# A hybrid decoder layer on one core: the order of the first loads, and eight opening weight halves run as two sweeps over four banks

## The chip, the core and the metric

The kernel runs on one core of one Trainium2 chip. The metric is the device time of one execution in microseconds (us); of several executions the median is taken. Engines are named as in the profile: PE is TensorE, DVE VectorE, ACT ScalarE, POOL GpSimd, SP SyncE. SP computes nothing here; it issues nearly all of the transfers, in the order of its program. Loads are counted in MiB of 1,048,576 bytes.

## The reference, cut to what matters

One layer over 256 tokens of width 2048, all float32. A vector c makes six modulation vectors of 2048 through the matrix `w_mod`; two of them (shift and scale) act on the normalized x ahead of the first projection:

```python
c_act = jax.nn.silu(c)
mod = (c_act @ w_mod[l] + b_mod[l])[:, None, :]
sh1, sc1, g1, sh2, sc2, g2 = jnp.split(mod, 6, axis=-1)
h = rms_norm(x, norm1_g[l]) * (1.0 + sc1) + sh1
(fq, fk, fv, ff, nq, kc, vc, ksl, vsl, kwn, vwn, ng, ca, cg) = split_in(h @ w_in[l])
...
x = x + g1 * (mixed @ w_out[l])
h = rms_norm(x, norm2_g[l]) * (1.0 + sc2) + sh2
x = x + g2 * (jnp.square(jax.nn.relu(h @ w_mlp1[l])) @ w_mlp2[l])
return rms_norm(x, final_g)
```

`mixed` joins two attentions and a convolution. The change touches the program up to the first part of `h @ w_in`.

## The kernel before

Float32 products are made of three matmuls on split operands. Each operand is the sum of a high part (rounded, ACT makes it) and a low part (the rest, DVE makes it): high times high, high times low, low times high.

**Weights.** The columns of `w_in` stand in eleven groups of 512 (CA, CG, FV, FE, NQ, NS, NC, FA, FB, FC, and a narrow TL). A quarter is 512 rows of a group, one load of 1 MiB into one of four buffers `raw0` to `raw3`. A half is half of a quarter, 256 rows: ACT writes its high part to one of four `w_hi` (`weight_hi`, L637), DVE its low part to one of four `w_lo` (`weight_lo`, L1288), and PE runs 24 matmuls on it (`feature_rows`, L891 to L893, or `token_rows`, L914 to L916). In the text, h0, h1, ... are the halves in PE's order. `UNITS` lists which quarters follow each other into the same accumulator. There are four of these, bank pairs `pair[0]` to `pair[3]`. The first four units are quarter 0 of CA, CG, FV and FE, one in each pair, so that h0 and h1 are both halves of the first quarter of CA, h2 and h3 of CG, and so on. ACT may convert half n when PE has done half n - 4 (`pe_half`).

**Modulation.** A chunk m of `w_mod` is 1 MiB and gives 128 numbers: DVE multiplies it with the activated c and sums over a row (`modulation_column`, L1295). Chunks 0 to 3 make shift and scale of the first 256 features of h, chunks 4 to 7 of the next 256. Chunks 0 to 7, here m0 to m7, are loaded into the `raw` buffers ahead of all weights. Later ones (m8 and on) go to two buffers `mod_raw`, and DVE works them off between its weight halves at the turns that `MODS_AT` lists. Every engine walks over one list of turns. At turn n ACT and DVE prepare half n, and PE, three slots later in its own list, multiplies it. DVE's turns 7 and 8, in order: low part of h7, m11, m12; then a small memset and the low parts of h8 and h9.

**h.** ACT squares x (L618), DVE makes the inverse root (`inverse_rms`), ACT scales x (L625), PE transposes it in eight blocks through two PSUM banks (L979) and ACT copies each block out (`xn_t`, L629). For each 256 features ACT then applies shift and scale and makes the high part (`scale_shift`, L648 and L651) and DVE the low part (`split_h`, L1345). h0 needs the first such piece, h1 the second.

**Loads.** SP waits on semaphores before it issues a load whose buffer is in use: for m4 to m7 and the first four quarters on `mod_step`, which counts the chunks that DVE has done; for later quarters on `lo_done`, which counts the halves that DVE has split; for later chunks on `mod_step` again. A load that waits holds up all that stand behind it on SP. Ten small constants are issued by ACT (L605). ACT also writes the table of relative positions to DRAM (`bias_rows`, L660) at turn 5 and waits for its arrival before its first copy of a result (`copy_result`, L666).

## Time and profile before

| | |
|---|---|
| median of 3 executions | 1260.14 us (1258.65 to 1262.6) |
| the profiled execution | 1256.01 us |
| its span, first to last instruction | 1254.3 us, so 1.7 us lie around it |
| PE / weight loads of PE / DVE / ACT busy | 93% / 81% / 72% / 48% |
| mean granted clock of PE | 0.971 of 2.4 GHz |

A busy share is a mean over the whole layer. The change lies in the first 70 us, where PE has its longest idle stretches, so the windows of those 70 us and what ends each wait in them matter more than the totals.

### The profile page before, as it was taken

Reading aid. Unit: us, or ns where it says so; the run is one execution under the profiler, and the core shown is the slowest. Engines: PE = TensorE matmul, PEld = TensorE weight load, DVE = VectorE, ACT = ScalarE, POOL = GpSimd, SP = SyncE. Lnnn points to the kernel's source line nnn. Section 1 sums busy time; section 2 is a strip of 40 time slices with the busy share of each in tenths; the row PEclk is TensorE's granted clock in tenths of the full one; section 3 lists DMA queues with packets and bytes.
Section 4 is the critical chain, followed back from the end, with each engine's and each line's share of the span. In section 5 each row is a group of like instructions: output and inputs, shape, how many; then the busy total and the mean of one; then the engine's idle time right before and its main releaser. Section 6 shows DMA issues by size and latency. Waiting matters only on the chain.

```text
span 1254.3 us, 17205 instructions
## 1 busy us (share of the span) xinstructions
PE 1160.6 (93%) x6775; PEld 1014.0 (81%) x6775; DVE 903.1 (72%) x1009; ACT 597.7 (48%) x858; POOL 8.6 (1%) x24
## 2 busy tenths in 40 slices
PE   2789999898998998599999999999999999999995
PEld 1789998887876777599988888888888888888784
DVE  5788898999998867698766567554576545667674
ACT  5554546875645543544434344434444433444442
POOL 2000000000000000000000000000000000000000
PEclk9899999899898999799999999999999999999998
DMA  9999998456875556298576655556565556664441
GB/s 367 416 368 370 364 383 346 156 200 239 310 240 206 230 196 242 102 377 338 221 270 234 247 224 205 196 202 231 208 256 184 191 201 226 243 234 168 168 168 67
DMA packets 45913, 307.17 MB, mean 245 GB/s; under 512 B 6349, under 2 KB 7961, under 8 KB 9241
## 3 DMA queue, kind: packets, MB, share of 16 engines
q1 hardware_dynamic: 42768, 303.50, 64.5%
q10 hardware_dynamic: 3016, 2.78, 0.8%
q8 instruction: 43, 0.70, 0.2%
q14 instruction: 22, 0.17, 0.0%
q0 software_dynamic: 64, 0.02, 0.0%
HBM read 304.16 MB, written 2.12 MB: 244 GB/s over the span
## 4 chain that ended last, share of the span: by engine, by line
PE 72%; DVE 14%; issue 5%; ACT 5%; DMA 3%; ACTq 0%; SPq 0%; DVEq 0%
PE quad L901 14%; PE quad L914 11%; PE quad L916 11%; PE quad L915 11%; PE quad L903 7%; PE quad L891 5%; PE quad L892 5%; PE quad L893 5%; DVE w_lo L1288 3%; DVE mod_raw L1295 2%; DVE conv_y L1382 2%; DMA mod_raw<-in_w_mod 2%; ACT w_hi L637 2%; DMA raw<-in_w_mod 1%; ACT score L688 1%
## 5 line engine op out<-in xcount | busy, mean ns | idle before, releaser
L1288 DVE TENSOR_TENSOR w_lo<-raw,w_hi 128x1024 fp32r<-128x1024 f32 (+1 forms) x376 | 450.5, 1207 | 276.3 <-ACT w_hi L637 276.0
L637 ACT ACTIVATE w_hi<-raw 128x1024 fp32r<-128x1024 f32 (+1 forms) x376 | 391.8, 1046 | 464.6 <-PE quad L916 237.1
L901 PE MATMUL quad<-act,w_hi 128*128 128x512 f32 x768 | 271.5, 399 | 0.0
L891 PE MATMUL quad<-act,w_hi 128*128 128x256 f32 x768 | 225.2, 293 | 15.9 <-DVE w_lo L1288 10.7
L892 PE MATMUL quad<-act,w_hi 128*128 128x256 f32 x768 | 222.1, 289 | 0.0
L893 PE MATMUL quad<-act,w_lo 128*128 128x256 f32 x768 | 221.9, 289 | 0.0
L903 PE MATMUL quad<-act,w_lo 128*128 128x256 f32 x768 | 215.7, 281 | 0.0
L914 PE MATMUL quad<-w_hi,u_hi 128*128 128x512 f32 x512 | 199.6, 390 | 0.0
L915 PE MATMUL quad<-w_lo,u_hi 128*128 128x512 f32 x512 | 199.2, 389 | 0.0
L916 PE MATMUL quad<-w_hi,u_lo 128*128 128x512 f32 x512 | 199.2, 389 | 0.0
L901 PEld LDWEIGHTS quad<-act,w_hi 128*128 128x128 f32 x768 | 144.3, 188 | 36.0
L891 PEld LDWEIGHTS quad<-act,w_hi 128*128 128x128 f32 x768 | 152.6, 199 | 19.8 <-issue 14.8
L892 PEld LDWEIGHTS quad<-act,w_hi 128*128 128x128 f32 x768 | 152.4, 198 | 0.1
L893 PEld LDWEIGHTS quad<-act,w_lo 128*128 128x128 f32 x768 | 152.1, 198 | 0.0
L903 PEld LDWEIGHTS quad<-act,w_lo 128*128 128x128 f32 x768 | 145.1, 189 | 0.1
L1295 DVE CUSTOM_DVE_ANT_0 mod_raw<-mod_raw,acc 128x2048 f32<-128x2048 f32 x56 | 128.0, 2286 | 11.4 <-DMA mod_raw<-in_w_mod 11.1
L914 PEld LDWEIGHTS quad<-w_hi,u_hi 128*128 128x128 f32 x512 | 96.1, 188 | 20.3 <-issue 0.2
L915 PEld LDWEIGHTS quad<-w_lo,u_hi 128*128 128x128 f32 x512 | 96.1, 188 | 20.0 <-issue 0.2
L916 PEld LDWEIGHTS quad<-w_hi,u_lo 128*128 128x128 f32 x512 | 96.1, 188 | 19.9
L1306 DVE SCALAR_TENSOR_TENSOR acc<-mod_raw,c_act,acc 128x2048 f32<-128x2048 f32 x32 | 75.0, 2345 | 0.2 <-DMA mod_raw<-in_w_mod 0.2
L688 ACT ACTIVATE score<-score,neg_max 128x128 f32<-128x128 f32 x72 | 31.9, 444 | 51.6 <-DVE neg_max L1410 51.6
L676 ACT ACTIVATE conv_p<-conv_in,convw 128x256 f32<-128x256 f32 x108 | 45.8, 496 | 9.0 <-DVE conv_y L1382 9.0
(257 smaller groups left out, 1081.0 us busy)
## 6 DMA issues: line engine op xcount, KB each, us to landing
raw<-in_w_main SPq DMA_DIRECT2D x184, 1024.0 KB, 4.8
mod_raw<-in_w_mod SPq DMA_DIRECT2D x88, 1024.0 KB, 6.5
...
out<-raw SPq DMA_DIRECT2D x4, 512.0 KB, 4.0
...
```

The lines of the kernel that those rows point to most:

```text
L637: A(w_hi[j % 4][:, 0:2 * width], block_half(raw, j, width), ACT.Copy).then_inc(hi_done, 1)
L891: mm(out, hi, act_hi[:, k, :], start=begin and m % 2 == 0, stop=False, skip_group_check=True)
L892: mm(out, hi, act_lo[:, k, :], start=False, stop=False, skip_group_check=True)
L893: last = mm(out, lo, act_hi[:, k, :], start=False, stop=end, skip_group_check=True)
L901: mm(out, w_hi[j % 4][:, cols], act_both[:, k, :, :].rearrange("p h t -> p (h t)"), start=begin, stop=False, skip_group_check=True)
L903: last = mm(out[:, 0:S], w_lo[j % 4][:, cols], act_hi[:, k, :], start=False, stop=end, skip_group_check=True)
L914: mm(out, t_hi, hi, start=begin, stop=False)
L915: mm(out, t_hi, lo, start=False, stop=False)
L916: last = mm(out, t_lo, hi, start=False, stop=end)
L1288: TTn(w_lo[j % 4][:, 0:2 * width], block_half(raw, j, width), w_hi[j % 4][:, 0:2 * width].bitcast(f32), ALU.subtract).then_inc(lo_done, 1)
L1295: v.tensor_tensor_reduce(out=src[:, :], in0=src[:, :], in1=acc[0][:, :], scale=1.0, scalar=0.0, op0=ALU.mult, op1=ALU.add, accum_out=m_col ...
L1306: STT(out, src[:, :], c_act[:, bass.ds(k, 1)], out, ALU.mult, ALU.add).then_inc(mod_step, 1)
```

## The change

Four things are changed together.

- **Order of the first loads.** SP issues the row of c, m0 and m1 (now into `mod_raw`), x, m2 and m3 (into `raw2` and `raw3`), the first halves of quarters 0 and 1 (0.5 MiB each), the ten small constants (moved from ACT), then m4, first half 2, m5, first half 3, m6, and the second halves of quarters 0 to 3 around m7. After these come m8 and m9.
- **Two sweeps.** The first eight halves go over the four bank pairs twice: h0 to h3 are now the first halves of CA, CG, FV and FE and need only the first piece of h. h4 to h7 are their second halves and need the second. The results of the four units are now copied at turns 8 to 11 (before: 5, 7, 9, 11), and the table of positions is written ahead of them.
- **x.** It is squared as each of its two row tiles arrives, and scaled and transposed in two halves of its features; the second four blocks are transposed between h1 and h2.
- **DVE and ACT orders** for m0 to m7 and h0 to h3 are written out by hand. A quarter 4 to 7 is issued when the low part of h4 to h7, each the last user of its buffer, is made. m8, m9 and m10 are worked off at turns 4, 5 and 6, m11 and m12 still at turn 7.

```diff
+HALF_AT[0:8] = [(n % 4, n // 4) for n in range(8)]
+UNIT_END = [5 + u if u < 4 else FIRST_HALF[u + 1] for u in range(N_UNITS)]
+FIRST_MODS = 4
+RAW_LOADS = (1, 1, 2, 2)
...
-MODS_AT = {2 * q + 1: 1 + (q in (3, 8)) for q in range(30) if q != 14}
+MODS_AT = {4: 1, 6: 1} | {2 * q + 1: 1 + (q in (3, 8)) for q in range(2, 30) if q != 14}
...
-            def weights_in(n):
-
-                sp.wait_ge(mod_step, MOD_FIRST - 4 + n + 2)
-                sp.dma_start(raw[n][:, :], main_d[n, :, :]).then_inc(raw_full[n], 16)
+            def first_part(n):
+
+                if n in (2, 3):
+                    sp.wait_ge(mod_step, n + 2)
+                sp.dma_start(first_half(n), main_d[n % 4, :, n // 4 * 2 * GW:(n // 4 + 1) * 2 * GW])\
+                    .then_inc(part_in[n] if n < 4 else raw_full[n - 4], 16)
 
             def modulation(m, slot):
 
-                if not (isinstance(m, int) and m < MOD_FIRST + 2):
-                    sp.wait_ge(mod_step, m)
+                sp.wait_ge(mod_step, m - 2 if isinstance(m, int) and m < 6 else m)
...
+            sp.dma_start(c_col[:, :], c_d).then_inc(c_in, 16)
             sp.dma_start(acc[0][:, :], crow_d.to_broadcast([P, D])).then_inc(c_in, 16)
-            sp.dma_start(c_col[:, :], c_d).then_inc(c_in, 16)
-            sp.dma_start(n1[:, :], n1_d).then_inc(c_in, 16)
-            sp.dma_start(b_col[:, :], bcol_d).then_inc(c_in, 16)
+            for m in range(2):
+                sp.dma_start(mod_raw[m][:, :], wmod_d[m, :, :]).then_inc(mod_full[m], 16)
             for tt in range(TT):
-                sp.dma_start(x_a[:, tt, :], x_d[tt * P:(tt + 1) * P, :]).then_inc(x_in, 16)
-            for m in range(MOD_FIRST):
-                if m >= 4:
-                    sp.wait_ge(mod_step, m - 4 + 2)
-                sp.dma_start(raw[m % 4][:, :], wmod_d[m, :, :]).then_inc(raw_full[m % 4], 16)
+                sp.dma_start(x_a[:, tt, :], x_d[tt * P:(tt + 1) * P, :]).then_inc(x_in[tt], 16)
+            sp.dma_start(n1[:, :], n1_d).then_inc(col_in, 16)
+            sp.dma_start(b_col[:, :], bcol_d).then_inc(col_in, 16)
+            for m in range(2, 4):
+                sp.dma_start(raw[m][:, :], wmod_d[m, :, :]).then_inc(raw_full[m], 16)
+            first_part(0)
+            first_part(1)
+            loads = [(n2[:, :], n2_d),
...
+            for dst, src in loads:
+                sp.dma_start(dst, src).then_inc(small_in, 16)
+            modulation(4, 0)
+            first_part(2)
+            modulation(5, 1)
+            first_part(3)
+            modulation(6, 0)
+            first_part(4)
+            modulation(7, 1)
+            for n in range(5, 8):
+                first_part(n)
+            for n in range(2):
+                modulation(MOD_FIRST + n, n)
...
-                sp.wait_ge(lo_done, 2 * (r - 4) + 2)
+                sp.wait_ge(lo_done, r + 1 if r < 8 else 2 * (r - 4) + 2)
...
-                if half is not None and half % 2:
+                if half is not None and 4 <= half < 8:
+                    next_quarter(half)
+                elif half is not None and half >= 8 and half % 2:
...
+            def scale_x(half):
+
+                act.wait_ge(rstd_ok, 1)
+                cols = slice(half * (D // 2), (half + 1) * (D // 2))
+                for tt in range(TT):
+                    A(x_a[:, tt, cols], x_a[:, tt, cols], ACT.Copy, scale=rstd[:, tt:tt + 1]).then_inc(xn_ok, 1)
...
-                act.wait_ge(pe_half, FIRST_HALF[u + 1])
+                act.wait_ge(pe_half, UNIT_END[u])
...
-            for b in range(2):
-                scale_shift(b)
-                weight_hi_in(b)
+            scale_x(0)
+            copy_x(0)
+            copy_x(1)
+            first_hi(0)
+            scale_shift(0)
+            first_hi(1)
+            copy_x(2)
+            copy_x(3)
+            first_hi(2)
+            scale_x(1)
+            first_hi(3)
+            for b in range(4, 8):
+                copy_x(b)
+            bias_rows()
+            scale_shift(1)
...
-            pe.wait_ge(xn_ok, TT)
-            for b in range(KT // 2):
+            def x_transposes(b):
+
+                pe.wait_ge(xn_ok, 2 if b < 4 else 4)
...
+            for b in range(4):
+                x_transposes(b)
...
                 if slot == 2:
 
+                    for b in range(4, 8):
+                        x_transposes(b)
                     pe.wait_ge(small_in, 16 * N_SMALL)
                     mm(spare[0:NNSA, 0:S], rel_t[:, :], onehot[:, :], start=True, stop=True).then_inc(bias_ps, 1)
-                if slot == FIRST_HALF[2]:
                     pe.wait_ge(xt_ok, KT // 2)
-                if slot == FIRST_HALF[3]:
+                if slot == 3:
...
-            for m in range(MOD_FIRST):
-                if m == 2:
-                    inverse_rms(0)
-                modulation_column(m, raw[m % 4], raw_full[m % 4], 16 * (m // 4 + 1))
-                if m % 4 == 3:
-                    scale_shift(m // 2 - 1, 2, m + 1, n1, m // 2 - 1)
+                if n < 8:
+                    dve.wait_ge(hi_done, n + 1)
+                    TTn(w_lo[n % 4][:, :], first_half(n), w_hi[n % 4][:, :].bitcast(f32), ALU.subtract)\
+                        .then_inc(lo_done, 1)
+                else:
+                    weight_lo(n // 8, n % 8, TAIL if n < IN_HALVES and UNITS[HALF_AT[n][0]][0] == TL else GW)
+
+            modulation_column(0, mod_raw[0], mod_full[0], 16)
+            modulation_column(1, mod_raw[1], mod_full[1], 16)
+            inverse_rms(0)
+            modulation_column(2, raw[2], raw_full[2], 16)
+            modulation_column(3, raw[3], raw_full[3], 16)
+            dve.wait_ge(col_in, 2 * 16)
+            scale_shift(0, 2, 4, n1, 0)
+            weight_lo_in(0)
+            split_h(0)
+            weight_lo_in(1)
+            modulation_column(4, mod_raw[0], mod_full[0], 32)
+            weight_lo_in(2)
+            modulation_column(5, mod_raw[1], mod_full[1], 32)
+            weight_lo_in(3)
+            modulation_column(6, mod_raw[0], mod_full[0], 48)
+            modulation_column(7, mod_raw[1], mod_full[1], 48)
+            scale_shift(2, 2, 8, n1, 2)
+            split_h(1)```

DVE at its start, where the first weight half follows the modulation chunks (`w_lo` is a weight's low part, `act` the low part of h, and ISA rows are a chunk's product and its read-out). Before:

```order
L1320 TENSOR_TENSOR m_sum<-m_col,b_col 128x4
L1321 SCALAR_TENSOR_TENSOR scale_h<-m_sum,n1 128x2
L1345 TENSOR_TENSOR act_49<-h_f0_63,act_49 128x2x256
L1288 TENSOR_TENSOR w_lo0<-raw0,w_hi0 128x1024
L1345 TENSOR_TENSOR act_49<-h_f1_64,act_49 128x2x256
L1288 TENSOR_TENSOR w_lo1<-raw0,w_hi1 128x1024
L1295 ISA mod_raw0,m_col<-mod_raw0,acc0 128x2048
```

And now, from the first sum of four chunks on:

```order
L1373 TENSOR_TENSOR m_sum<-m_col,b_col 128x4
L1374 SCALAR_TENSOR_TENSOR scale_h<-m_sum,n1 128x2
L1404 TENSOR_TENSOR w_lo0<-raw0,w_hi0 128x1024
L1398 TENSOR_TENSOR act_49<-h_f0_63,act_49 128x2x256
L1404 TENSOR_TENSOR w_lo1<-raw1,w_hi1 128x1024
L1348 ISA mod_raw0,m_col<-mod_raw0,acc0 128x2048
L1348 ISA m_col 128x1
L1404 TENSOR_TENSOR w_lo2<-raw2,w_hi2 128x1024
```

In the rows of before the sum is that of m4 to m7, in the rows of now that of m0 to m3: h0's low part stands ahead of four chunks that it used to follow, and m4 (the first ISA row of now) stands behind the low part of h1.

SP around the first weights, before:

```order
L490 DMA raw2<-in_w_mod 128x2048
L490 DMA raw3<-in_w_mod 128x2048
L472 DMA raw0<-in_w_main 128x2048
L478 DMA mod_raw0<-in_w_mod 128x2048
L472 DMA raw1<-in_w_main 128x2048
L478 DMA mod_raw1<-in_w_mod 128x2048
L472 DMA raw2<-in_w_main 128x2048
L472 DMA raw3<-in_w_main 128x2048
L499 DMA raw0<-in_w_main 128x2048
L478 DMA mod_raw0<-in_w_mod 128x2048
```

And now, from first half 3 on (128x1024 is a half of a quarter):

```order
L483 DMA raw3<-in_w_main 128x1024
L489 DMA mod_raw0<-in_w_mod 128x2048
L483 DMA raw0<-in_w_main 128x1024
L489 DMA mod_raw1<-in_w_mod 128x2048
L483 DMA raw1<-in_w_main 128x1024
L483 DMA raw2<-in_w_main 128x1024
L483 DMA raw3<-in_w_main 128x1024
L489 DMA mod_raw0<-in_w_mod 128x2048
L489 DMA mod_raw1<-in_w_mod 128x2048
L531 DMA raw0<-in_w_main 128x2048
L489 DMA mod_raw0<-in_w_mod 128x2048
L531 DMA raw1<-in_w_main 128x2048
```

The second row of now is m6, which waits for m4's buffer; the second halves, m7, m8 and m9 stand behind it.

DVE at turns 7 and 8, now (before, the same rows stand in the same order under their old line numbers):

```order
L1404 TENSOR_TENSOR w_lo3<-raw3,w_hi3 128x1024
L1348 ISA mod_raw1,m_col<-mod_raw1,acc0 128x2048
L1348 ISA m_col 128x1
L1373 TENSOR_TENSOR m_sum<-m_col,b_col 128x4
L1374 SCALAR_TENSOR_TENSOR scale_h<-m_sum,n1 128x2
L1348 ISA mod_raw0,m_col<-mod_raw0,acc0 128x2048
L1348 ISA m_col 128x1
L1592 MEMSET conv_in_70 128x4x30
L1341 TENSOR_TENSOR w_lo0<-raw0,w_hi0 128x1024
```

The product in the sixth row is m12, and h8's low part in the last row stands behind it, as it did before.

## Rows read from the trace of the kernel before

**Rows 1.** Page of the profile: span; busy us (share) and instructions by engine
```profile
span 1254.3 us, 17205 instructions
PE 1160.6 (93%) x6775; PEld 1014.0 (81%) x6775; DVE 903.1 (72%) x1009; ACT 597.7 (48%) x858; POOL 8.6 (1%) x24
```

**Rows 2.** Windows: busy us (instructions) of PE, PEld, DVE, ACT, POOL; PEclk, DMA share, GB/s
```profile
30.00:40.00 10.00, 3.65 (x20) 2.97 (x20) 8.47 (x12) 7.14 (x12) 0.00 (x0) 0.68 1.02 423
40.00:50.00 10.00, 10.00 (x67) 9.44 (x67) 8.20 (x8) 3.44 (x4) 0.00 (x0) 0.81 1.01 420
60.00:70.00 10.00, 6.60 (x30) 5.48 (x29) 8.00 (x10) 5.10 (x8) 0.00 (x0) 0.89 0.98 382
80.00:90.00 10.00, 10.00 (x86) 10.00 (x85) 8.12 (x10) 6.63 (x9) 0.00 (x0) 1.00 0.94 338
...
68.00:71.50 3.50, 3.50 (x18) 3.50 (x19) 3.30 (x4) 0.00 (x0) 0.00 (x0) 0.54 0.95 379
```

**Rows 3.** Chain that ended last, up to h8: start us, us, what
```profile
27.85 7.58 DMA raw<-in_w_main
...
37.92 0.55 PE quad L891
...
57.58 6.52 DMA mod_raw<-in_w_mod
66.59 1.24 DVE w_lo L1288
```

**Rows 4.** Timeline, DVE: start us, us, what, [idle before <-releaser]
```profile
13.81 2.29 DVE L1295 CUSTOM_DVE_ANT_0 raw<-raw,acc 128x2048 f32<-128x2048 f32 x1 [3.65 <-DMA raw<-in_w_mod]
19.22 0.16 DVE L1326 TENSOR_REDUCE newton<-ssq 128x2 f32<-128x8 f32 x1
20.64 0.16 DVE L1334 TENSOR_TENSOR rstd<-rstd,newton 128x2 f32<-128x2 f32 x1
64.12 2.29 DVE L1295 CUSTOM_DVE_ANT_0 mod_raw<-mod_raw,acc 128x2048 f32<-128x2048 f32 x1 [1.69 <-DMA mod_raw<-in_w_mod]
```

**Rows 5.** Timeline, ACT: same columns
```profile
12.27 0.61 ACT L618 ACTIVATE sq_a<-x_a 128x512 bf16<-128x512 f32 x1
20.84 3.90 ACT L625 ACTIVATE x_a<-x_a,rstd 128x2048 f32<-128x2048 f32 x2 [1.02 <-DVE rstd L1334]
26.00 0.60 ACT L629 ACTIVATE xn_t<-quad 128x512 f32<-128x512 f32 x1 [1.27 <-PE quad L979]
26.85 0.60 ACT L629 ACTIVATE xn_t<-quad 128x512 f32<-128x512 f32 x1 [0.26 <-PE quad L979]
36.42 1.08 ACT L648 ACTIVATE h_f<-xn_t,m_sum,scale_h 128x256 f32<-128x256 f32 x2
38.07 1.04 ACT L637 ACTIVATE w_hi<-raw 128x1024 fp32r<-128x1024 f32 x1
40.42 2.00 ACT L637 ACTIVATE w_hi<-raw 128x1024 fp32r<-128x1024 f32 x2 [1.31 <-DMA raw<-in_w_main]
45.40 1.06 ACT L637 ACTIVATE w_hi<-raw 128x1024 fp32r<-128x1024 f32 x1 [2.98 <-DMA raw<-in_w_main]
52.11 1.02 ACT L666 ACTIVATE conv_in<-quad 128x1024 f32<-128x1024 f32 x1 [4.59 <-DMA bias_scratch<-bias_p]
```

**Rows 6.** Timeline, SP's issues; then us from issue to landing (source of L478)
```profile
55.37 0.33 SPq L499 DMA_DIRECT2D raw<-in_w_main  x1
57.58 0.33 SPq L478 DMA_DIRECT2D mod_raw<-in_w_mod  x1
DMA to landing us min/median/max: 5.2/7.1/12.3
```

**Rows 7.** Timeline, PE: the last matmul of h7 and the first of h8
```profile
64.17 0.39 PE L916 MATMUL quad<-w_hi,act 128*128 128x512 f32 x1
67.96 0.55 PE L891 MATMUL quad<-act,w_hi 128*128 128x256 f32 x1 [3.40 <-DVE w_lo L1288]
```

**Rows 8.** Page, issues: KB of each, median us from issue to landing
```profile
out<-raw SPq DMA_DIRECT2D x4, 512.0 KB, 4.0
```

More of the change, by code:

```diff
@@ L336, in build @@
         c_in = sem("c_in")
+        col_in = sem("col_in")
+        part_in = [sem(f"part_in{i}") for i in range(4)]
         small_in = sem("small_in")
-        x_in = sem("x_in")
+        x_in = [sem(f"x_in{i}") for i in range(TT)]
         consts = sem("consts")
@@ L613, in _, with copy_x @@
             sqrt_table(0)
-            act.wait_ge(x_in, 16 * TT)
-            for n in range(4 * TT):
-                tt, cg = n % TT, n // TT
-                A(sq_a[:, n * GW // 2:(n + 1) * GW // 2].bitcast(mybir.dt.bfloat16),
-                  x_a[:, tt, cg * GW:(cg + 1) * GW], ACT.Square, accum_out=ssq[:, 0, tt, cg:cg + 1])\
-                    .then_inc(act_sq, 1)
+            for tt in range(TT):
+                act.wait_ge(x_in[tt], 16)
+                for cg in range(4):
+                    n = 4 * tt + cg
+                    A(sq_a[:, n * GW // 2:(n + 1) * GW // 2].bitcast(mybir.dt.bfloat16),
+                      x_a[:, tt, cg * GW:(cg + 1) * GW], ACT.Square, accum_out=ssq[:, 0, tt, cg:cg + 1])\
+                        .then_inc(act_sq, 1)
             act.wait_ge(dve_ms, 1)
             A(root[:, :], mean_sq[:, :], ACT.Sqrt).then_inc(act_root, 1)
-            act.wait_ge(rstd_ok, 1)
-            for tt in range(TT):
-                A(x_a[:, tt, :], x_a[:, tt, :], ACT.Copy, scale=rstd[:, tt:tt + 1]).then_inc(xn_ok, 1)
-            for b in range(KT // 2):
+            def scale_x(half):
+                act.wait_ge(rstd_ok, 1)
+                cols = slice(half * (D // 2), (half + 1) * (D // 2))
+                for tt in range(TT):
+                    A(x_a[:, tt, cols], x_a[:, tt, cols], ACT.Copy, scale=rstd[:, tt:tt + 1]).then_inc(xn_ok, 1)
+            def copy_x(b):
                 act.wait_ge(xt_ps, b + 1)
@@ L630, in _, with first_hi @@
                   ACT.Copy).then_inc(xt_ok, 1)
+            def first_hi(n):
+                act.wait_ge(part_in[n], 16)
+                A(w_hi[n][:, :], first_half(n), ACT.Copy).then_inc(hi_done, 1)
             def weight_hi(g, j, width=GW):
[L634 to L636 removed]
+                act.wait_ge(raw_full[j // 2], (g + RAW_LOADS[j // 2]) * 16)
+                act.wait_ge(pe_half, g * 8 + j - 3)
                 A(w_hi[j % 4][:, 0:2 * width], block_half(raw, j, width), ACT.Copy).then_inc(hi_done, 1)
             def weight_hi_in(n):
[L640 removed]
+                if n < 8:
+                    act.wait_ge(raw_full[n % 4], 16 * RAW_LOADS[n % 4])
+                    act.wait_ge(pe_half, n - 3)
+                    A(w_hi[n % 4][:, :], first_half(n), ACT.Copy).then_inc(hi_done, 1)
+                else:
+                    weight_hi(n // 8, n % 8, TAIL if n < IN_HALVES and UNITS[HALF_AT[n][0]][0] == TL else GW)
             def scale_shift(b):
                 act.wait_ge(col_ok, b + 1)
+                act.wait_ge(xt_ok, b + 1)
                 if b >= 2:
@@ L971, in _ @@
             pe.wait_ge(consts, 1)
-            pe.wait_ge(xn_ok, TT)
-            for b in range(KT // 2):
+            def x_transposes(b):
+                pe.wait_ge(xn_ok, 2 if b < 4 else 4)
                 if b >= 2:
@@ L1219, in normalized @@
                 half = 1 if b < KT // 4 else 2
-                pe.wait_ge(xn_ok, TT + half)
+                pe.wait_ge(xn_ok, 2 * TT + half)
                 pe.wait_ge(xn_act, half)
@@ L1309, in later_modulation @@
                 n = m - MOD_FIRST
-                source = (mod_raw[n % 2], mod_full[n % 2], 16 * (n // 2 + 1))
+                source = (mod_raw[n % 2], mod_full[n % 2], 16 * (n // 2 + 4))
                 if MOD_G1 <= m < MOD_H2:
@@ L1517, in _ @@
             for turn, (half, step) in enumerate(TURNS):
-                if turn < 2:
-                    split_h(turn)
+                if turn < FIRST_MODS:
+                    continue
                 if turn == 8:
@@ L1530, in _ @@
                 for u in ADDED:
-                    if turn == FIRST_HALF[u + 1] + 3:
+                    if turn == UNIT_END[u] + 3:
                         add_result(u)
```

39 lines of the change are left out of this document (15 added, 24 removed).

## The prediction

> **What bounds the kernel now.** I read the page first, then the windows of the first 80 us, the chain of waits up to h8, and last the timelines of DVE, ACT, SP and PE in that stretch.
>
> The page says that PE is busy for 93% of 1254.3 us [rows 1], so a change of the start can only win what PE idles there. Its first weight matmul starts at 37.92 [rows 3], and it idles again from the end of h7 (64.17) to h8 at 67.96 [rows 7]. From h8 on it is full: 86 matmuls in 10 us at 80 us, which is 24, one half, in 2.8 us [rows 2]. All the work behind h8 is the same before and after. So the change is worth what it moves the start of h8, plus what the clock does around it.
>
> What sets h8? In the chain the last steps ahead of it are a transfer into `mod_raw`, issued at 57.58 and landed 6.5 us later, and h8's low part at 66.59 [rows 3]. That transfer is m12: DVE stands idle until it lands at 64.12, multiplies it, and only then splits h8 [rows 4]. From m12's landing to PE's h8 it is 3.84 us.
>
> And what sets m12? The transfers share the DMA engines, whose share is 1.01 or 1.02 from 30 to 50 us at 420 to 423 GB/s [rows 2]. ACT's waits show the pace. The row of c, two tiles of x, m0 to m7 and quarter 0 are 12 MiB, and the 12th lands at 35.4 [rows 3]; m8 and quarter 1 (14) by 40.42, m9 and quarter 2 (16) by 45.40 [rows 5]. That is 2.49 us per MiB. m0, the 4th, lands at 13.81 [rows 4]; eight more at 2.49 would make 33.7, so 1.7 us are lost on the way. m12 is the 23rd: at 2.49 from the 12th it would land at 62.8, and it landed at 64.12. The missing 1.3 us follow an SP that had issued quarter 6 only at 55.37 and m12 at 57.58 [rows 6].
>
> **The change, part by part.** After the change the loads up to m12 are again the row of c, x, m0 to m12, eight halves of quarters (4 MiB) and quarters 4 to 6: 23 MiB. Nothing is removed ahead of m12, and DVE's h8 still stands behind it. PE's earlier h0 is therefore worth nothing by itself. The term that decides is whether the queue of transfers runs dry more or less often than before, so I walk through it.
>
> *Up to h0.* x's second tile is the 5th MiB and lands at 13.8 + 2.49 = 16.3. Its four squares, 0.61 each [rows 5], end at 18.8; the inverse root took 19.22 to 20.80, 1.6 us [rows 4], so 20.4. Half of x is scaled in 3.90 / 2 = 1.95: 22.4. Before, the first block's copy began 1.3 us after the scaling and the next 0.85 after that [rows 5]: 23.7 and 24.5, done 25.1. h0's high part, 1.06: 26.2 (its 0.5 MiB, number 7.5, landed at 22.5). m2 and m3 are done by 20.4 + 2 x 2.2 + 0.6 for the sums = 25.4. Shift, scale and high part took 36.42 to 38.07, 1.65 us [rows 5]: 27.8. DVE's low part, 0.7, lets PE begin h0 at 28.6, 9.3 us earlier than now.
>
> *First pause.* ACT makes h1's high part by 28.9, DVE its low part (1.24 [rows 3]) by 30.1 and then m4 by 32.3. m6 needs m4's buffer and is issued at 32.3. The 11 MiB issued ahead of it have landed by 13.8 + 7 x 2.49 + 1.7 = 33.0, and no load of this kind lands less than 5.2 us after its issue [rows 6]. So m6, the 12th, lands at 37.5, where an unbroken queue gives 35.5: 2.0 us lost. All later loads stand behind m6 on SP. How long the ten constants, now in SP's own queue, hold it is shown by no row; anything from nothing to about 2 us is hidden here, as m6's time comes from DVE and not from the queue. I take the 1.7 of before.
>
> *Second pause.* m7 lands at 41.2, m8 at 47.5, m9 at 50.0 (numbers 13.5, 16, 17); their issues, at 35.7, 39.7 and 43.4, are in time. m7 is done at 43.4, the sums at 43.9, ACT's second piece at 45.6, h4's high part at 46.7 and its low part at 47.9. Only then is `raw0` free, since h0 and h4 share it now, and quarter 4 is issued, 7.5 us later than before. It lands at 47.9 + 5.2 = 53.1, where the queue could have had it at 52.5: 0.6 us.
>
> *To m12.* Five more MiB (m10, quarter 5, m11, quarter 6, m12) put m12 at 53.1 + 12.5 = 65.6. The issues are in time: m10 at 50.1, quarter 5 at 51.3, m11 at 53.5, quarter 6 at 54.7, m12 at 57.9. Of the 1.3 us that m12 lost before I have replaced the cause by the second pause but not the thinner rate (382 GB/s from 60 to 70 us [rows 2]). Between 0 and 1.3 more I take 0.5, nearer to 0, as m12 now stands behind a longer queue: 66.1. h8 follows at 66.1 + 3.84 = 69.9 to 70.0, against 67.96: **+2.0 us**.
>
> *Hidden edits.* The copies of results at turns 8 to 11 lie on ACT while h8 waits for m12. The transposes of the last four blocks now stand between h1 and h2 on PE, some 3.4 us at 0.85 per block. With a low clock in h0 and h1 (5.6 us each from 28.6) they end by 43.2, with a recovering one by 41; ACT needs them before its second piece of h, which waits for m7's sums until 43.9 anyway. That cover is thin: each us beyond it delays quarter 4 and h8 by as much. The early table of positions frees ACT of a wait of 4.6 us at turn 5 [rows 5]; it delayed h5 to h7 and quarter 6, and is part of the 1.3.
>
> *Clock.* PE is done with h7 near 62.0 (h7's low part 59.1, one half 2.8), so it idles 8 us before h8, not 3.4. After 3.4 idle us the grant was 0.54 of 2.4 GHz from 68.0 to 71.5 [rows 2], so low for 3.2 us, a loss of 1.6. At the first weights, after a longer rest, it stayed low from 37.9 to 43.8 (0.81 over 40 to 50 is 3.8 us at half speed [rows 2]), a loss of 2.9. So this costs between 0 and 1.3 us more. I take 0, from the row of the same place, and keep 1.3 for the range.
>
> **Sum.** 1256.0 (the profiled execution) + 2.0 = 1258.0. The median of the runs shown is 4.1 above that execution, so the forecast is 1260.1 + 2.0 = 1262.1.
>
> **A rule of the skill.** The half loads are 0.5 MiB. The 512 KB stores at the end land in 4.0 us [rows 8] and a 1 MiB load at the least in 5.2: 1.2 for 0.5 MiB, the pace of the queue, and 2.8 that don't shrink. If each of the four extra transfers paid 2.8 in the queue, m12 would land 11 us later: 1273. Against it: full loads already land 2.49 apart, with no such part between them. The Trainium skill (DMA: Bandwidth & Descriptors, section Bandwidth) asks for transfers of at least 1 MiB for most of the peak rate; by that rule this rival would have its cause, while the trace's queue agrees with it only for a lone transfer.
>
> **The rivals.**
> - *The queue never pauses.* If m4 is done sooner than I walk, or the engines are still busy when m6 comes, m12 lands at 62.8 and h8 starts 1.3 us earlier than now; a clock that doesn't fall gives 1.6 more. 1257.2 to 1259.5. For it: DMA's share is full in the windows of before. Against it: m6's issue hangs on eight steps of ACT and DVE.
> - *The early start is kept.* If m12 is not bound by bytes but by DVE's turn, h8 follows h7 and up to 9.3 us are won: 1250.8. It decides from the point where 23 MiB could be there by 55 us; at 423 GB/s they alone take 57 us. Even a part beyond 3.8 us would need it.
> - *Late chain and cold clock.* ACT's steps to h1 run 1 to 2 us longer than the sum, m12 loses its full 1.3 again and the clock its 1.3: 1264 to 1266.5.
>
> **How the numbers follow.** Forecast case 0.48; no pause 0.15; early start kept 0.08; late chain and clock 0.25; half loads paying their own 0.04. A measurement here tells about 0.3%, 3.8 us, from no change, so the first two are "same": 0.63. Faster 0.08, slower 0.29. The range leaves out the early start, the half loads and the ends of the others: 1258.0 to 1266.0.
>
> **What the new profile would show.** PE's first weight matmul near 28.6; m6 issued near 32.3 with a dip of the transfer rate at 31 to 34 and a smaller one near 49; DVE idle ahead of m12, landing near 66; h8 near 70, after some 8 idle us of PE; from there the same rows as before, 2 us later. The prediction is wrong if DVE doesn't wait for m12, if the rate shows no dip, or if the time behind h8 is no longer that of before.

## The result: 0.3% slower, and where the profile after shows it

The changed kernel takes 1263.42 us (median of 22 runs, 1260.2 to 1272.36), the kernel before 1259.51 on the same chip (22 runs, 1257.53 to 1264.07). The ratio is 1.0029, 95% interval 1.0018 to 1.0040: by it 3.65 us more, 2.3 to 5.0. I had forecast 1262.1, 2.0 more, in a range of 1258 to 1266. The sign came, and so did the two pauses of the queue and the wait for m12; the size was too small.

The page of the profile after, first the span, then busy us and instructions by engine (against [rows 1]):

```profile
span 1264.6 us, 17222 instructions
PE 1165.7 (92%) x6775; PEld 1017.4 (80%) x6775; DVE 903.6 (71%) x1009; ACT 598.1 (47%) x860; POOL 8.6 (1%) x24
```

This span is 10.3 us longer than that of before, far more than the medians differ. The chain that ended last shows the first piece of it (start us, us, what; against [rows 3]):

```profile
32.05 5.73 DMA mod_raw<-in_w_mod
...
40.13 9.42 DMA mod_raw<-in_w_mod
...
51.90 7.24 DMA mod_raw<-in_w_mod
...
61.49 7.58 DMA mod_raw<-in_w_mod
...
71.56 1.24 DVE w_lo L1341
```

Before, one transfer into `mod_raw` stood in this stretch of the chain; now there are four, m6, m8, m10 and m12. Each is issued when DVE has worked off the chunk two before it (m4, m6, m8, m10), and DVE then waits for it. The stage has become a loop of two buffers. PE's timeline after (against [rows 7]), with the idle time ahead in brackets:

```profile
28.39 0.39 PE L938 MATMUL quad<-act,w_hi 128*128 128x256 f32 x1 [2.34 <-DVE act L1398]
48.55 0.35 PE L938 MATMUL quad<-act,w_hi 128*128 128x256 f32 x1 [3.91 <-DVE w_lo L1404]
62.75 0.47 PE L961 MATMUL quad<-w_hi,act 128*128 128x512 f32 x1 [3.24 <-DVE w_lo L1404]
72.93 0.55 PE L938 MATMUL quad<-act,w_hi 128*128 128x256 f32 x1 [5.60 <-DVE w_lo L1341]
152.79 0.36 PE L938 MATMUL quad<-act,w_hi 128*128 128x256 f32 x1 [0.74 <-DVE w_lo L1341]
```

h0 starts 9.5 us earlier than before and h8 5.0 us later. Between them lie two new waits (3.91 and 3.24), a longer one ahead of h8 (5.60 against 3.40) and the transposes that now stand behind h1. SP's timeline and DVE's landings (the same columns) show two pauses of the queue, and a start of it that is held up:

```profile
18.21 2.42 SPq L511 DMA_DIRECT2D pos_t<-in_pos  x2
20.68 0.61 SPq L489 DMA_DIRECT2D mod_raw<-in_w_mod  x1
...
32.05 0.33 SPq L489 DMA_DIRECT2D mod_raw<-in_w_mod  x1
...
48.43 0.33 SPq L531 DMA_DIRECT2D raw<-in_w_main  x1
...
61.49 0.33 SPq L489 DMA_DIRECT2D mod_raw<-in_w_mod  x1
```

```profile
37.81 2.29 DVE L1348 CUSTOM_DVE_ANT_0 mod_raw<-mod_raw,acc 128x2048 f32<-128x2048 f32 x1 [1.30 <-DMA mod_raw<-in_w_mod]
41.72 2.29 DVE L1348 CUSTOM_DVE_ANT_0 mod_raw<-mod_raw,acc 128x2048 f32<-128x2048 f32 x1 [1.61 <-DMA mod_raw<-in_w_mod]
49.57 2.29 DVE L1348 CUSTOM_DVE_ANT_0 mod_raw<-mod_raw,acc 128x2048 f32<-128x2048 f32 x1 [1.17 <-DMA mod_raw<-in_w_mod]
59.16 2.29 DVE L1348 CUSTOM_DVE_ANT_0 mod_raw<-mod_raw,acc 128x2048 f32<-128x2048 f32 x1 [2.81 <-DMA mod_raw<-in_w_mod]
69.09 2.29 DVE L1348 CUSTOM_DVE_ANT_0 mod_raw<-mod_raw,acc 128x2048 f32<-128x2048 f32 x1 [2.27 <-DMA mod_raw<-in_w_mod]
```

The ten constants keep SP until m4's issue at 20.68; m6 goes out at 32.05 and lands at 37.81, m7 lands at 41.72, m8 at 49.57, m10 at 59.16, m12 at 69.09.

How much is that? The last column of the windows is the rate at which bytes moved. Times the length of a window it is a count of bytes, and this count is what I compare most below. Before:

```profile
0.00:28.00 28.00, 3.12 (x15) 2.78 (x16) 15.12 (x22) 15.18 (x27) 6.31 (x22) 1.00 0.92 360
28.00:48.00 20.00, 13.65 (x77) 12.04 (x76) 18.47 (x19) 11.97 (x18) 0.00 (x0) 0.74 1.02 421
48.00:60.00 12.00, 11.66 (x71) 10.11 (x70) 6.08 (x7) 7.19 (x8) 0.00 (x0) 1.00 1.01 412
0.00:60.00 60.00, 28.44 (x159) 24.92 (x160) 39.67 (x46) 34.33 (x52) 6.31 (x22) 0.91 0.97 391
```

After:

```profile
0.00:28.00 28.00, 3.60 (x16) 2.96 (x16) 14.36 (x21) 16.38 (x31) 6.32 (x22) 1.00 0.90 351
28.00:48.00 20.00, 15.75 (x90) 13.50 (x90) 14.69 (x16) 11.79 (x17) 0.00 (x0) 0.91 0.98 378
48.00:60.00 12.00, 10.70 (x60) 9.43 (x60) 8.02 (x8) 6.39 (x8) 0.00 (x0) 0.86 0.91 345
0.00:60.00 60.00, 30.06 (x166) 25.89 (x166) 37.08 (x43) 34.56 (x54) 6.32 (x22) 0.94 0.93 359
```

By 60 us the changed kernel has moved (391 - 359) x 60 = 1.9 MB less. At the full queue's 420 GB/s [rows 2] that is 4.6 us: 0.6 of it up to 28 us, 2.0 from 28 to 48 (the first pause), 1.9 from 48 to 60 (the second). h8 is 5.0 us late. Further on, h35 (27 halves behind h8; every profile has a short wait ahead of it) starts at 152.79, against 148.09 in the profile before: 4.7 late.

### The profile page after: what moved, and what is told of

Same layout as the page of the kernel before. It is cut to its first block, busy times and chain, and to the rows that moved or that the text cites. A ratio compares the mean times of both kernels' runs of the same rounds, so it can differ in the third digit from the quotient of the medians.

```text
span 1264.6 us, 17222 instructions
## 1 busy us (share of the span) xinstructions
PE 1165.7 (92%) x6775; PEld 1017.4 (80%) x6775; DVE 903.6 (71%) x1009; ACT 598.1 (47%) x860; POOL 8.6 (1%) x24
## 4 chain that ended last, share of the span: by engine, by line
PE 65%; DVE 17%; DMA 8%; ACT 5%; issue 5%; SPq 0%; ACTq 0%; DVEq 0%
PE quad L948 14%; PE quad L961 10%; PE quad L963 10%; PE quad L962 10%; PE quad L950 7%; DMA mod_raw<-in_w_mod 6%; DVE w_lo L1341 4%; DVE mod_raw L1348 4%; PE quad L938 3%; PE quad L939 3%; PE quad L940 3%; DVE conv_y L1452 2%; DVE acc L1359 1%; ACT w_hi L668 1%; ACT score L737 1%
## 5 line engine op out<-in xcount | busy, mean ns | idle before, releaser
L1341 DVE TENSOR_TENSOR w_lo<-raw,w_hi 128x1024 fp32r<-128x1024 f32 (+1 forms) x368 | 440.9, 1207 | 273.1 <-ACT w_hi L668 272.7
L668 ACT ACTIVATE w_hi<-raw 128x1024 fp32r<-128x1024 f32 (+1 forms) x368 | 383.8, 1046 | 463.3 <-PE quad L963 237.7
L948 PE MATMUL quad<-act,w_hi 128*128 128x512 f32 x768 | 271.5, 399 | 0.0
L938 PE MATMUL quad<-act,w_hi 128*128 128x256 f32 x768 | 225.6, 294 | 18.6 <-DVE w_lo L1341 7.0
L961 PE MATMUL quad<-w_hi,u_hi 128*128 128x512 f32 x512 | 199.6, 390 | 0.0
L948 PEld LDWEIGHTS quad<-act,w_hi 128*128 128x128 f32 x768 | 144.3, 188 | 36.0
L938 PEld LDWEIGHTS quad<-act,w_hi 128*128 128x128 f32 x768 | 153.1, 199 | 22.7 <-issue 14.8
L1348 DVE CUSTOM_DVE_ANT_0 mod_raw<-mod_raw,acc 128x2048 f32<-128x2048 f32 x62 | 141.7, 2287 | 18.9 <-DMA mod_raw<-in_w_mod 18.4
L961 PEld LDWEIGHTS quad<-w_hi,u_hi 128*128 128x128 f32 x512 | 96.1, 188 | 20.3 <-issue 0.2
## 6 DMA issues: line engine op xcount, KB each, us to landing
raw<-in_w_main SPq DMA_DIRECT2D x8, 512.0 KB, 9.6
out<-raw SPq DMA_DIRECT2D x4, 512.0 KB, 4.0
```

The lines of the kernel that those rows point to most:

```text
L668: A(w_hi[j % 4][:, 0:2 * width], block_half(raw, j, width), ACT.Copy).then_inc(hi_done, 1)
L938: mm(out, hi, act_hi[:, k, :], start=begin and m % 2 == 0, stop=False, skip_group_check=True)
L948: mm(out, w_hi[j % 4][:, cols], act_both[:, k, :, :].rearrange("p h t -> p (h t)"), start=begin, stop=False, skip_group_check=True)
L961: mm(out, t_hi, hi, start=begin, stop=False)
L1341: TTn(w_lo[j % 4][:, 0:2 * width], block_half(raw, j, width), w_hi[j % 4][:, 0:2 * width].bitcast(f32), ALU.subtract).then_inc(lo_done, 1)
L1348: v.tensor_tensor_reduce(out=src[:, :], in0=src[:, :], in1=acc[0][:, :], scale=1.0, scalar=0.0, op0=ALU.mult, op1=ALU.add, accum_out=m_col ...
```

## The experiments

Theory A was at first my prediction's: h8's start decides, since all behind it is the same. After the first results it became: the stream of bytes decides, and what the queue loses in the first 60 us is not got back. The rivals stand in each expectation. Every ratio is to the kernel before on the same chip. The kernels of the first group (before 1260.94 us) change one thing of either kernel.

**m12 late, in the changed kernel.** m12 is taken out of turn 7 and put behind h8, so that h8 no longer waits for it.

```diff
-MODS_AT = {4: 1, 6: 1} | {2 * q + 1: 1 + (q in (3, 8)) for q in range(2, 30) if q != 14}
+MODS_AT = {4: 1, 6: 1, 8: 1} | {2 * q + 1: 1 + (q == 8) for q in range(2, 30) if q != 14}
```

> The changed kernel, with chunk m12 worked off at turn 8, behind the low part of h8, and no longer at turn 7 ahead of it. Theory A (h8 starts when m12 has landed and been multiplied, and the rest of the kernel follows h8 one to one): h8's low part now only waits for m11 (landed 64.1 in the changed kernel), so h8 starts near 68.2 and not 72.9, the idle stretch before it is shorter, and the median falls by 4.7 to 6 us, to 1257.5 to 1259. Theory B (the bytes gate the stage wherever m12 stands): PE is stopped some halves later by the same landing, a new wait of 3 us or more shows between h8 and h14, and the median falls by under 2 us.

Measured: 1263.78 us, ratio 1.0026 (1.0011 to 1.0041). PE's waits in it:

```profile
67.22 0.36 PE L938 MATMUL quad<-act,w_hi 128*128 128x256 f32 x1 [1.04 <-DVE w_lo L1341]
71.52 0.36 PE L938 MATMUL quad<-act,w_hi 128*128 128x256 f32 x1 [1.19 <-DVE w_lo L1341]
76.45 0.36 PE L938 MATMUL quad<-act,w_hi 128*128 128x256 f32 x1 [1.83 <-DVE w_lo L1341]
109.91 0.36 PE L938 MATMUL quad<-act,w_hi 128*128 128x256 f32 x1 [1.03 <-DVE w_lo L1341]
116.62 0.36 PE L938 MATMUL quad<-act,w_hi 128*128 128x256 f32 x1 [0.73 <-DVE w_lo L1341]
152.76 0.35 PE L938 MATMUL quad<-act,w_hi 128*128 128x256 f32 x1 [1.78 <-DVE w_lo L1341]
```

h8 starts at 67.22, 5.7 us earlier than after the change, and h35, which stood at 152.79, stands at 152.76. The gain is taken back by waits of half a dozen weight halves, none of them the single wait of 3 us or more that theory B expected. That h8's start decides one for one is refuted.

**The same in the kernel before.**

```diff
-MODS_AT = {2 * q + 1: 1 + (q in (3, 8)) for q in range(30) if q != 14}
+MODS_AT = {8: 1} | {2 * q + 1: 1 + (q == 8) for q in range(30) if q != 14}
```

> The kernel before, with the same edit alone (m12 at turn 8 behind h8's low part). Theory A: PE goes from h7 (ends 64.3) into h8 without a pause and the clock doesn't fall, so h8 starts 3.7 us earlier and another 1.6 us of half clock are saved: 1254 to 1256. Theory B: the wait comes back a few halves later, 1257.5 to 1259.5.

Measured: 1259.33 us, ratio 0.9990 (0.9974 to 1.0006). The wait of 3.40 us ahead of h8 [rows 7] is gone, h8 starts at 63.92, and waits of 1.14 at 68.08, 1.83 at 73.01, 1.17 at 97.45 and 1.23 at 107.33 have come. Not measurably faster, as theory B had it.

**The ten constants back on ACT's queue.**

```diff
-            for dst, src in loads:
-                sp.dma_start(dst, src).then_inc(small_in, 16)
...
+            for dst, src in loads:
+                act.dma_start(dst, src).then_inc(small_in, 16)
```

> The changed kernel, with the ten small constants issued by ACT again. Theory A (their place is hidden, since m6's issue at 32.1 comes from DVE's chain and not from the queue): h8 moves by under 1 us, the median stays within 1 us of 1263.4. Rival (they hold SP until 20.7 and thin the transfers to 256 to 316 GB/s between 20 and 26 us, and that delays all loads): h8 comes 1.5 to 2 us earlier, median near 1261.5.

Measured: 1265.47 us, ratio 1.0032 (1.0018 to 1.0046), h8 at 74.30, 350 GB/s up to 60 us against 359 after the change. Moving the constants back gains nothing, and both theories missed: h8 comes 1.4 us later. From 24 to 28 us the queue now runs at 419 GB/s where it ran at 328, but the first transposes come at 24.05 instead of 22.45 and m6 goes out at 33.65 instead of 32.05, and from 28 to 48 us the rate is 344 where it was 378. What the constants cost is not separated by this run.

**m6 into a buffer of its own.**

```diff
+        mod_x = at("mod_x", 28 * K, [P, D])
...
-            modulation(6, 0)
+            sp.dma_start(mod_x[:, :], wmod_d[6, :, :]).then_inc(mod_x_full, 16)
```

> The changed kernel, with chunk m6 in a buffer of its own that is free at that time, issued without a wait. Theory A (the first pause of the queue, at 32 us, is what m6's wait for m4's buffer costs): no dip at 32 to 34 us, m6 to m12 land about 2 us earlier, h8 near 71, median near 1261.5. Rival (the time is lost later, at quarter 4 behind h4's low part, whatever comes before): m7 lands earlier but m12 by under 0.7 us, and the median stays at 1263.

Measured: 1263.52 us, ratio 1.0020 (1.0005 to 1.0035), h8 at 72.18, 357 GB/s up to 60 us. SP's timeline says why so little came:

```profile
25.85 0.44 SPq L518 DMA_DIRECT2D mod_x<-in_w_mod  x1
26.33 0.47 SPq L485 DMA_DIRECT2D raw<-in_w_main  x1
36.35 0.33 SPq L491 DMA_DIRECT2D mod_raw<-in_w_mod  x1
```

m6 now goes out at 25.85, but m7 needs m5's buffer and goes out at 36.35, with the second halves behind it. The pause has moved from m6 to m7. m12 lands at 68.34, 0.75 us earlier than after the change, which is near what the rival expected.

The second group (before 1260.53 us) goes at the bytes themselves.

**m4 to m8 without a wait for the chunks of DVE's second round.** m4, m5 and m6 get spare buffers, so that m7 and m8 find `mod_raw` free.

```diff
+        mod_x = [in_hold(f"mod_x{i}", 8 * K * (i + 1), [P, D]) for i in range(3)]
...
-            modulation(4, 0)
+            spare_modulation(4)
```

> The changed kernel, with chunks m4, m5 and m6 in three buffers of their own (free memory at that time) and m7 and m8 in buffers that are free early, so that nothing from m4 to m8 waits for DVE's chain. Theory now held (the first 200 us go by the bytes that the transfers have moved: at 60 us the changed kernel is 1.9 MB or 4.6 us behind the kernel before, and that lag is still there at 200 us): the queue stays full from 26 to 48 us, the lag at 60 us shrinks to under 0.7 MB, h8 starts at 69.5 or earlier, and the median is that of the kernel before within 0.15% (ratio 0.9985 to 1.0015). Rival (the loss is PE's low clock and broken halves h0 to h7, or the half loads, not the pauses): the ratio stays at 1.002 to 1.003.

Measured: 1261.68 us, ratio 0.9997 (0.9980 to 1.0014). m8 is issued at 28.25, h8 starts at 70.05. The windows:

```profile
28.00:48.00 20.00, 17.85 (x98) 15.61 (x99) 15.66 (x17) 13.79 (x20) 0.00 (x0) 1.00 1.02 413
48.00:52.00 4.00, 2.79 (x24) 2.62 (x23) 4.00 (x4) 1.44 (x2) 0.00 (x0) 1.00 0.85 279
0.00:60.00 60.00, 29.97 (x167) 25.74 (x168) 39.60 (x45) 35.16 (x54) 6.33 (x22) 1.00 0.96 375
```

With the first pause filled (413 GB/s where 378 was) the ratio is that of no change. The second pause stays: after m8 the queue got nothing but m9, at 42.46, until h4's low part let quarter 4 go out at 46.86, and from 48 to 52 us it ran at 279 GB/s. So two parts of the theory missed: the lag at 60 us is 1.0 MB, not under 0.7, and h8 comes at 70.05, not by 69.5.

**2 MiB more, in the kernel before.** Two loads that nothing uses stand ahead of the first weights: only the stream is made later, by a known amount.

```diff
+            for n in range(2):
+                sp.dma_start(extra[:, n, :], wmod_d[n, :, :]).then_inc(extra_in, 16)
             for n in range(4):
                 weights_in(n)
```

> The kernel before, with two more loads of 1 MiB (chunks m0 and m1 once more, into memory that nobody reads) between m7 and the first weights. Theory of the bytes: every landing behind them is 5 us later, the halves up to 200 us too, and the median rises by 4 to 5.5 us (ratio 1.0032 to 1.0045). Rival (slack further on takes it up, so early loads are not what counts): PE is under 2 us later at 148 us and the ratio is below 1.002.

Measured: 1265.23 us, ratio 1.0042 (1.0024 to 1.0060), 5.3 us (3.0 to 7.6). 2 MiB are 2.1 MB, at 420 GB/s 5.0 us. So a lag of the stream does cost time; that it costs its whole length fits but isn't shown, as the interval is wide and the one profile has h8 4.7 us later than before and h35 only 3.5 us later.

**Half loads in the kernel before.** The first four quarters as eight loads of 0.5 MiB.

```diff
-                sp.dma_start(raw[n][:, :], main_d[n, :, :]).then_inc(raw_full[n], 16)
+                for k in range(2):
+                    cols = slice(k * 2 * GW, (k + 1) * 2 * GW)
+                    sp.dma_start(raw[n][:, cols], main_d[n, :, cols]).then_inc(raw_full[n], 16)
```

> The kernel before, with each of the first four quarters loaded as two loads of 0.5 MiB. If a half load costs a part that doesn't shrink (up to 2.8 us each in a lone transfer), the bytes at 60 us are behind by 1 MB or more and the ratio is above 1.003. Theory (in a filled queue only the bytes count): under 0.3 MB behind, ratio 0.9985 to 1.0015.

Measured: 1260.91 us, ratio 1.0001 (0.9985 to 1.0017), h8 at 68.18. In a full queue eight half loads cost nothing that can be measured in the time, and up to 60 us only 0.2 MB. The profile does come late further on:

```profile
150.63 0.35 PE L893 MATMUL quad<-act,w_hi 128*128 128x256 f32 x1 [1.85 <-DVE w_lo L1290]
```

That is h35, 2.5 us behind the first profile of before, with the median unmoved. The Trainium skill (DMA: Bandwidth & Descriptors, section Bandwidth) asks for transfers of at least 1 MiB; the ratio of this run shows no loss from going below it here.

**1 MiB less, in the kernel before.** The row of c is loaded once, 8 KB, and spread over the partitions by PE.

```diff
-            sp.dma_start(acc[0][:, :], crow_d.to_broadcast([P, D])).then_inc(c_in, 16)
+            sp.dma_start(acc[0][0:1, :], crow_d).then_inc(c_in, 16)
...
+                last = mm(quad[0][:, cg * GW:(cg + 1) * GW], ones[0:1, :], acc[0][0:1, cg * GW:(cg + 1) * GW],
+                          start=True, stop=True)
```

> The kernel before, with the row of c loaded once (8 KB) and spread over the partitions by four matmuls with ones, so that the first load of 1 MiB is gone. Theory of the bytes: everything in the queue comes 2.5 us earlier, as long as the first chunk is not held by the longer way to the activated c (some 1.5 us more), and the median falls by 1.5 to 2.5 us (ratio 0.998 to 0.9988). Rival (the start is bound by DVE's chain of chunks): no change, 0.9995 to 1.0005.

Measured: 1262.06 us, ratio 1.0005 (0.9990 to 1.0021): at the edge of what the rival had, and not the 1.5 to 2.5 us hoped for. PE's matmuls and DVE's first product:

```profile
4.07 7.16 PE L977 MATMUL quad<-acc,ones 1*128 1x512 f32 x8 [4.07 <-DMA b_col<-in_b_mod_cols]
```

```profile
13.18 0.18 DVE L1347 TENSOR_TENSOR c_act<-c_tmp,c_col 128x16 f32<-128x16 f32 x1 [13.18 <-ACT acc L600]
```

Spreading takes 7.16 us, and DVE begins at 13.18 instead of 7.79: the longer way costs 5.4 us, not some 1.5. From then on no chunk of m0 to m7 waits for its load; their buffers come free later, and the queue ran at 264 GB/s from 24 to 28 us, where it was 405 before. This is no clean test of the saving; here the bytes saved at the price of DVE's first product came back as a pause.

The third group (before 1260.13 us) closes the second pause too, and repeats both kernels as they are.

**m9 and m10 ahead of quarter 4.** On top of the spare buffers for m4 to m6.

```diff
-            modulation(9, 1)
+            sp.wait_ge(mod_step, 8)
+            sp.dma_start(mod_x[2][:, :], wmod_d[9, :, :]).then_inc(mod_x_full[2], 16)
+            sp.wait_ge(mod_step, 8)
+            sp.dma_start(mod_x[1][:, :], wmod_d[10, :, :]).then_inc(mod_x_full[1], 16)
```

> The changed kernel with m4, m5, m6 in spare buffers as in the run before, and now m9 and m10 in two of them again, so that both are issued ahead of quarter 4 and 2 MiB stand in the queue while quarter 4 waits for h4's low part: the second pause (279 GB/s from 48 to 52 us in that run) should go. Theory A (what counts is how far the stream of bytes lags, each pause adding to it): 22.9 to 23.4 MB by 60 us instead of 22.5, h8 1 to 2 us earlier than 70.05, and a ratio to the kernel before of 0.997 to 1.000, below the run with m4 to m6 alone (0.9997) by 0.0005 to 0.0015. Theory B (the whole loss came from the first pause and the rest is scatter between executions): the rate fills but the ratio stays at 0.9997 or above. Theory C (the constants in SP's queue hold the rest): the bytes by 60 us stay under 22.7.

Measured: 1260.38 us, ratio 1.0000 (0.9989 to 1.0011). Its windows and two of PE's waits:

```profile
28.00:48.00 20.00, 18.23 (x101) 15.99 (x102) 16.54 (x17) 13.95 (x20) 0.00 (x0) 1.00 1.02 420
48.00:60.00 12.00, 10.81 (x64) 8.89 (x62) 9.71 (x10) 5.01 (x6) 0.00 (x0) 1.00 1.02 423
0.00:60.00 60.00, 32.85 (x178) 27.88 (x178) 40.26 (x46) 34.96 (x54) 6.31 (x22) 1.00 0.97 389
```

```profile
68.07 0.55 PE L948 MATMUL quad<-act,w_hi 128*128 128x256 f32 x1 [7.96 <-DVE w_lo L1351]
148.16 0.35 PE L948 MATMUL quad<-act,w_hi 128*128 128x256 f32 x1 [0.81 <-DVE w_lo L1351]
```

Both pauses are gone, the rate is that of before, and h8 and h35 are back within 0.2 us of before. This kernel begins its weights at 28.81, some 9 us before the kernel before, and is no faster. That the constants hold the rest (theory C) fell with 23.3 MB by 60 us. In bytes and in h8 theory A came; the ratio is theory B's, no lower than that of the spare buffers for m4 to m6 alone. So what the second pause costs in time is not shown. What both pauses cost together is: on the same chip the changed kernel, repeated below, takes 1263.36 us, 3.0 more than this one, and the two intervals (0.9989 to 1.0011 and 1.0011 to 1.0042) touch only at their ends.

**Both kernels again.**

> The kernel before, unchanged, as one more contestant: what a ratio of a kernel to itself comes out as, and a second profile of it. Theory A (the profile of before shown is an early one by chance; runs whose median is that of before stand at 149.8 to 151.6 and 239 to 240.5): this profile has its weight half near 148 to 151 us at 149 or later and its wait near 236.40 at 238 to 240. Theory B (before's profile is typical, and the others' places are owed to their edits): 148.1 and 236.4 again within 0.5. Ratio 0.999 to 1.001 in both.

> The changed kernel, unchanged, once more: whether 5 us more behind 148 us (which the shown profile of it has between 330 and 530 us) belong to the change or to that one execution. Theory A (scatter of one execution): h8 near 72.9 and the place at 152.8 come again within 1 us, but the lag at the norm behind the attention (526.90 in the shown profile) comes out at 521 to 525, and the span at 1259 to 1262. Theory B (the late start makes later stages miss their transfers by more): 526 to 528 and a span of 1264 again. Ratio 1.002 to 1.004 in both.

Measured: before again 1259.65 us, ratio 0.9992 (0.9979 to 1.0006); after again 1263.36 us, ratio 1.0026 (1.0011 to 1.0042). PE's waits, before again:

```profile
68.03 0.55 PE L891 MATMUL quad<-act,w_hi 128*128 128x256 f32 x1 [3.72 <-DVE w_lo L1288]
148.47 0.35 PE L891 MATMUL quad<-act,w_hi 128*128 128x256 f32 x1 [0.66 <-DVE w_lo L1288]
237.05 0.39 PE L891 MATMUL quad<-act,w_hi 128*128 128x256 f32 x1 [3.74 <-DVE z_t L1389]
```

And after again:

```profile
72.41 0.55 PE L938 MATMUL quad<-act,w_hi 128*128 128x256 f32 x1 [7.13 <-DVE w_lo L1341]
153.04 0.36 PE L938 MATMUL quad<-act,w_hi 128*128 128x256 f32 x1 [0.83 <-DVE w_lo L1341]
241.55 0.41 PE L938 MATMUL quad<-act,w_hi 128*128 128x256 f32 x1 [3.72 <-DVE z_t L1459]
```

The kernel before came as theory B had it up to 148.47, and at 237.05 between the two theories, nearer to B; the changed kernel came within 0.6 us of its first profile up to there, and its norm behind the attention, at 525.55, lies between the two theories. In this pair the lag is 4.4 at h8, 4.6 at h35, 4.5 at 241.55 and 5.3 at the norm (525.55 against 520.22), and the spans, 1263.0 and 1258.6, differ by 4.4. So here the lag is made before h8 and is still there at the end. The rest of the 10.3 us between the first two profiles is scatter of single executions: the first profile of before ran 4.3 us shorter than its second, with h8 at the same place within 0.1.

All runs in one table, in the order of the bytes. MB by 60 us is the rate of that window times 60. The columns h35 and `z_t` are two later places of PE: the start of h35, and the first matmul behind the wait for `z_t`. All places are from one profile each, while the ratio is from 12 executions or more.

| kernel | GB/s to 60 us | MB by 60 us | h8 | h35 | `z_t` | ratio |
|---|---|---|---|---|---|---|
| before (first, again) | 391, 388 | 23.5, 23.3 | 67.96, 68.03 | 148.09, 148.47 | 236.40, 237.05 | 0.9992 (again) |
| m12 late (before) | 391 | 23.5 | 63.92 | 148.03 | 237.32 | 0.9990 |
| both pauses filled | 389 | 23.3 | 68.07 | 148.16 | 237.32 | 1.0000 |
| half loads (before) | 387 | 23.2 | 68.18 | 150.63 | 240.36 | 1.0001 |
| c by PE (before) | 362 | 21.7, and 1.0 saved | 69.74 | 149.77 | 239.39 | 1.0005 |
| first pause filled | 375 | 22.5 | 70.05 | 151.58 | 240.49 | 0.9997 |
| m12 late (changed) | 362 | 21.7 | 67.22 | 152.76 | 241.07 | 1.0026 |
| after (first, again) | 359, 360 | 21.5, 21.6 | 72.93, 72.41 | 152.79, 153.04 | 241.47, 241.55 | 1.0029, 1.0026 |
| before and 2 MiB | 393 | 23.6, of use 21.5 | 72.66 | 151.61 | 240.14 | 1.0042 |
| m6 alone | 357 | 21.4 | 72.18 | 151.72 | 240.41 | 1.0020 |
| constants on ACT | 350 | 21.0 | 74.30 | 154.30 | 242.66 | 1.0032 |

The ratio goes with the bytes and not with h8: in both kernels m12 late moved h8 by 4 to 6 us and left bytes, h35 and ratio where they were. All kernels that are 1.7 MB or more behind have a ratio of 1.0020 to 1.0042; those up to 1.0 MB behind can't be told from 1. Between them the order is not that of the lag: the first pause filled and the half loads are 2.5 to 3.5 us late at h35, and their medians don't show it.

## Why the prediction was right in kind and short in size

- **What bounds.** "The term that decides is whether the queue of transfers runs dry more or less often than before" held. The sentence ahead of it in the argument, that the change is worth what it moves the start of h8, did not: with m12 late h8 moved by 5.7 us and the time by nothing that can be told (1.0026 against 1.0029 and 1.0026). Both went together in my sum because m12, on which h8 waited, was a marker of the stream. The wait at h8 is where the lag shows, not what makes it.
- **How much the hit is worth.** The range of 8 us also held no change at all, so that the time fell into it says little. And two misses partly cancel: h8 came 5.0 us late where I had 2.0, but the time rose by 3.65 and not by all that h8 moved. That the total is off by only 1.65 is in part luck. The sharper signs are the two pauses, DVE's wait for m12, and the way from m12's landing to h8, 69.09 to 72.93, which is the 3.84 us of before.
- **Up to h0.** 28.6 forecast, 28.39 and 28.77 measured. PE's early start is worth nothing, as forecast; the kernel with both pauses filled shows it without the pauses.
- **First pause.** m6 issued at 32.3, landed at 37.5, 2.0 us lost: measured 32.05, 37.81, and (421 - 378) x 20 / 420 = 2.0 us (2.7 between the repeated profiles, 423 and 367 GB/s). That step was right.
- **Constants.** "Anything from nothing to about 2 us is hidden": SP was free at 20.68, 8.0 us after m4's buffer was (DVE was done with m0 at 12.7), and from 24 to 28 us the rate was 328 GB/s where it was 405 before. Over the first 28 us 0.6 us of bytes were missing, a small term that I had set to nothing. Whether the constants are its cause is open: with them back on ACT the rate to 28 us was 349 GB/s, no better than 351.
- **Second pause.** This is the term that was mis-sized. I took 0.6 us for quarter 4 and 0.5 for the thinner rate. Quarter 4 was issued at 48.43, near the 47.9 forecast, but it landed only at 55.98, where ACT waited for it, and not at 53.1 (in the repeated profile it was there by 54.46):

```profile
55.98 1.06 ACT L668 ACTIVATE w_hi<-raw 128x1024 fp32r<-128x1024 f32 x1 [1.71 <-DMA raw<-in_w_main]
```

m8 landed at 49.57 instead of 47.5, m10 at 59.16 instead of the 55.6 that the walk gives, m12 at 69.09 instead of 66.1, and from 48 to 60 us 1.9 us of bytes were missing (0.9 between the repeated profiles, 398 and 367). The walk let each transfer land when its turn in bytes had come, or 5.2 us after its issue. The ten issues of L489 in the first 70 us took 5.7 to 10.2 us to land, 7.8 in the middle. What makes them longer isn't shown. Nor is 5.2 us a least of these loads, as I had read [rows 6]: that is the least of one line in the first 80 us, and over the whole trace of before the same line has 4.7.
- **The credit for m12.** I let the 1.3 us that m12 lost before fall away. But by 60 us the kernel before had lost almost none of it: 412 GB/s from 48 to 60 us (398 in its second profile). Its thin stretch came later, 382 GB/s from 60 to 70 us [rows 2], where the changed kernel runs at 422 and pays at 346 from 70 to 80.
- **The clock.** The grant from 70 to 80 us is 0.66, 6.8 us at half speed if the rest is full, against 0.94 in the same window before (0.60 and 0.82 in the repeated profiles). PE idled 5.6 us before h8 and not 8, because h7, which I had done near 62.0, began only at 62.75. I had taken 0 of 0 to 1.3. It cost nothing that can be told: with m12 late the grant from 70 to 80 us is 1.00, and h35 starts at the same 152.8. As far as these two profiles show, where bytes decided a lower clock only took from PE's waits.
- **Rivals.** That the queue never pauses fell. The early start was not kept: 23 MiB were not there by 55 us, and DVE waited 2.27 us for m12. That half loads pay 2.8 us each fell with the ratio of 1.0001. The late chain with a cold clock would have given 1264 to 1266.5, and 1263.42 lies between it and the forecast, but by another road: ACT's steps came on time.

**What stays open.** The kernel with only the first pause filled still lacks 1 MB at 60 us, some 2.4 us, and its ratio of 0.9997 (0.9980 to 1.0014) leaves room for no more than 1.8. The half loads are the same case from the other side, 2.5 us late at h35 with a ratio of 1.0001 (0.9985 to 1.0017). Whether such a lag is got back further on, or belongs to the one execution profiled, isn't shown; a second profile of either kernel would tell. What the ten constants cost in SP's queue wasn't isolated, since moving them shifted other work too.
